# Prompt attention in 30 steps beside the samples' pages; keys transposed by VectorE in 32x32 blocks, scores in twelve 32x32 tiles at once

## The reference, cut to what matters

```python
# prompt: 512 queries, 512 keys
sc = einsum('bqhd,bkhd->bhqk', qi, k) * scale
sc = sc + ci[..., :, None] - c_k[:, :, None, :]          # c: running sum of log forget values
p = softmax(where(causal, sc, NEG_INF)); out = einsum('bhqk,bkhd->bqhd', p, v)
# sample: 8 queries, 2048 past keys in 16 pages of 128, found by a page table, and 8 new ones
r_past = cumsum(lf_past, reverse=True) - lf_past
s_past = einsum('bqhd,bkhd->bhqk', q, k_past) * scale + cq[..., :, None] + r_past[:, :, None, :]
p = softmax(concatenate([s_past, s_new], -1))
out = einsum('bhqk,bkhd->bqhd', p, concatenate([v_past, v]))
```

## Time and profile before

| | us |
|---|---|
| median of 3 runs | 2106.8 (2106.39 to 2113.93) |
| span of the profiled execution | 2106.6 |
| TensorE busy | 1840.3 (87%) |
| VectorE busy | 982.8 (47%) |
| ScalarE busy | 537.1 (25%) |
| GpSimd busy | 172.2 (8%) |
| TensorE in the chain that ended last | 74% of the span |
| DMA, mean over the span | 106 GB/s |

### The profile page before, as it was taken

How to read it: one execution, slowest core, us unless ns; L and a number is a source line. 1 busy time by engine, 2 the same in 40 slices (tenths; PEclk the granted TensorE clock), 3 DMA queues, 4 the chain that set the end, 5 groups by cost and what they waited for, 6 DMA issues and landing times.

```text
span 2106.6 us, 36927 instructions
## 1 busy us (share of the span) xinstructions
PE 1840.3 (87%) x13959; PEld 1610.9 (76%) x13959; DVE 982.8 (47%) x1689; ACT 537.1 (25%) x880; POOL 172.2 (8%) x332
## 2 busy tenths in 40 slices
PE   5999466899999999799766788888878899999998
PEld 4876345799999999699634456566557799999997
DVE  5396965533333222776457864444433533333222
ACT  3210233322222111433222323222312322222110
POOL 1010000000000000444100001122220000000000
PEclk9999867999999999999878769999988999999999
DMA  3210121222222322223421027788873222223221
GB/s 113 63 38 30 40 76 61 59 80 85 84 80 81 95 83 71 64 75 87 159 91 61 1 84 276 283 290 312 302 231 97 60 80 86 83 80 91 83 82 58
DMA packets 231243, 224.30 MB, mean 106 GB/s; under 512 B 12114, under 2 KB 199588, under 8 KB 231162
## 3 DMA queue, kind: packets, MB, share of 16 engines
q1 hardware_dynamic: 210736, 150.49, 23.1%
q0 software_dynamic: 19008, 69.43, 9.5%
q10 hardware_dynamic: 1418, 3.29, 0.5%
HBM read 215.37 MB, written 7.80 MB: 106 GB/s over the span
## 4 chain that ended last, share of the span: by engine, by line
PE 74%; DVE 14%; ACT 4%; DMA 3%; issue 3%; POOLq 0%; ACTq 0%; DVEq 0%; POOL 0%
PE ps L1335 54%; PE ps L1708 5%; PE ps L1544 3%; DMA vring<-in_cache_fox_v_dram 3%; PE ps L1720 2%; PE ps L1317 2%; PE ps L1746 2%; DVE tmp L382 1%; DVE stat L468 1%; PE ps L1725 1%; ACT prob L1046 1%; DVE prob L459 1%; DVE prob L494 1%; DVE yc L687 1%; DVE aL L386 1%
## 5 line engine op out<-in xcount | busy, mean ns | idle before, releaser
L1335 PE MATMUL ps<-aH,wH 128*128 128x288 f32 x2224 | 487.5, 301 | 51.8 <-DVE aL L386 34.6
L1335 PE MATMUL ps<-aL,wH 128*128 128x288 f32 x2224 | 480.3, 298 | 0.0
L1335 PE MATMUL ps<-aH,wL 128*128 128x288 f32 x2224 | 479.9, 298 | 0.0
L1335 PEld LDWEIGHTS ps<-aH,wH 128*128 128x128 f32 x2224 | 361.9, 191 | 61.2 <-issue 39.1
L363 DVE TENSOR_TENSOR wL<-raw,wH 128x1024 fp32r<-128x1024 f32 (+1 forms) x179 | 232.0, 1296 | 337.0 <-ACT wH L985 333.9
L1335 PEld LDWEIGHTS ps<-aL,wH 128*128 128x128 f32 x2224 | 362.3, 191 | 0.0
L1335 PEld LDWEIGHTS ps<-aH,wL 128*128 128x128 f32 x2224 | 362.2, 191 | 0.0
L985 ACT ACTIVATE wH<-raw 128x1024 fp32r<-128x1024 f32 (+1 forms) x179 | 198.8, 1111 | 386.6 <-PE ps L1335 358.1
L1335 PE MATMUL ps<-gH,wH 128*128 128x288 f32 x704 | 151.1, 296 | 4.8 <-DVE gL L605 4.8
L1335 PE MATMUL ps<-gH,wL 128*128 128x288 f32 x704 | 151.1, 295 | 0.0
L1335 PE MATMUL ps<-gL,wH 128*128 128x288 f32 x704 | 150.9, 295 | 0.0
(11 more groups left out here) (295 smaller groups left out, 1982.8 us busy)
## 6 DMA issues: line engine op xcount, KB each, us to landing
kring<-in_cache_fox_k_dram SPq DMA_DIRECT2D x128, 384.0 KB, 4.7
vring<-in_cache_fox_v_dram POOLq DMA_DIRECT2D x128, 384.0 KB, 5.2
raw<-in_w_gate_up_dram SPq DMA_DIRECT2D x88, 512.0 KB, 3.8
raw<-in_w_down_dram SPq DMA_DIRECT2D x32, 704.0 KB, 4.6
raw<-in_fox_w_in_dram SPq DMA_DIRECT2D x21, 512.0 KB, 3.9
raw<-in_w_out_dram SPq DMA_DIRECT2D x16, 512.0 KB, 3.8
raw<-in_conv_w_in_dram SPq DMA_DIRECT2D x14, 512.0 KB, 3.9
raw<-in_w_mem_kv_dram SPq DMA_DIRECT2D x8, 512.0 KB, 3.4
```

Source lines behind the costliest of these rows:

```text
L1335: mm = nc.tensor.matmul(ps[:, 2 * slot + h, 0:HT], weights[:, w], a[:, k0 + k, h * HT:(h + 1) * HT], start=(first and k == 0 and weights i ...
```

## The change

The prompt's 24 units become 30 steps (`fox_step`): a step has one head e and one or two parts, so that its scores always fill one bank of 512 columns: query tile 3 alone, tiles 0 and 2 of a head together, tile 1 of two heads together. The samples' 64 chunks become 32 slots of two chunks (512 keys, a quarter of a sample). Step s stands beside slot s in the order of every engine. All loops over samples are written out.

The keys are transposed by VectorE from SBUF to SBUF in 32x32 blocks (`KT`, two chunks to a slot, double), so TensorE's key transposes and both engines' copies out of PSUM go. A block has 32 channels, so a head is two blocks; partition group a holds the keys 32a to 32a + 31 of each page. `qx4` holds the queries in each of the four partition groups; scores are twelve tiles of 32x32, row group a and column group j, each into bank a, for 128 keys a tile; the forget rows follow as 32x32 tiles. All 2048 scores of a sample stay in the four banks 0 to 3: VectorE takes the maximum there, ScalarE's exponential reads them and writes S, and only then does the next sample's first slot write there. Banks 6 and 7 are taken in turn, in one order for all uses (`TURNS`). ScalarE takes over the copies of pT, pTs, the scaling and the queries (`spread`); GpSimd makes the forget rows (`forget_rows`) between its value loads; the forget stage stands beside the memory units (`forget(i)`). Both rings have three chunks.

```diff
-    RING = 4
+    RING = 3
+    SLOTS = NB * NCH // 2
+    SPB = SLOTS // NB
+    SPG = 2 * CPG
+    DQ = DH // 2
+    NBLK = CH // DQ
+    STEPS = 5 * HP
...
-    FOX_UNITS = [("fox", hp, t, (t + 1) * P) for hp in range(HP) for t in range(TT)]
+    def fox_step(i):
+        two, k = divmod(i, 5)
+        e, hp = two % 2, two - two % 2
+        parts = ([(0, 3, 0, SEQ)], [(1, 3, 0, SEQ)], [(0, 0, 0, P), (0, 2, P, 3 * P)], [(1, 0, 0, P), (1, 2, P, 3 * P)],
+                 [(0, 1, 0, 2 * P), (1, 1, 2 * P, 2 * P)])[k]
+        return k, e, [(n, hp + n, t, col, keys) for n, t, col, keys in parts]
...
+            def forget(i):
+                if i == 0:
+                    dve.wait_ge(lf_in, 16 * NB * NP)
+                    nc.vector.tensor_reduce(lftot[:], lfrow[:].rearrange("n (k h) -> n h k", h=NH), AX_X, ALU.add).then_inc(lftot_done, 1)
+                if i < 2 * (NH // 4):
+                    g = i % (NH // 4)
+                    bank = group()
...
+            def keys_T(s):
+                if s >= 2:
+                    dve.wait_ge(sc_done, s - 1)
+                for x in range(2):
+                    n = 2 * s + x
+                    dve.wait_ge(k_in[n % RING], 32 * (n // RING + 1))
+                    nc.vector.transpose(KT[s % 2][:, CPG * x:CPG * x + CPG, :].rearrange("p a n -> p (a n)"),
+                                        kring[n % RING][:].rearrange("p a n -> p (a n)")).then_inc(kt_done, 1)
...
+            def step_top(i):
+                k, e, parts = fox_step(i)
+                st = stat[:, 8 * (i % 2):8 * (i % 2) + 8]
+                pr = prob[:, i % 2, :]
+                if k == 0:
+                    for n in range(2):
+                        wait_taken(dve, ("ncb", i // 5, n))
+                dve.wait_ge(f_scores, i + 1)
+                for n, hp, t, col, keys in parts:
+                    last = nc.vector.scalar_tensor_tensor(out=pr[:, col:col + keys], in0=ps[:, 5, col:col + keys],
+                                                          scalar=ctok[:, t, 2 * hp + e:2 * hp + e + 1], in1=ncb[:, n, 0:keys],
+                                                          op0=ALU.add, op1=ALU.add)
+                link(last)
+                if k < 2:
+                    diagonal = pr[:, SEQ - P:SEQ]
+                    link(nc.vector.tensor_tensor(diagonal, diagonal, maskd[:], ALU.add))
+                else:
+                    first, by = (0, 3) if k < 4 else (1, 2)
+                    diagonal = pr.rearrange("p (a n) -> p a n", n=P)[:, first:TT:by, :]
+                    link(nc.vector.tensor_tensor(diagonal, diagonal, maskd[:].unsqueeze(1).broadcast_to([P, 2, P]), ALU.add))
+                for x, (n, hp, t, col, keys) in enumerate(parts):
+                    last = nc.vector.tensor_reduce(st[:, x:x + 1], pr[:, col:col + keys], AX_X, ALU.max, negate=True)
+                last.then_inc(f_max, 1)
+            def step_sums(i):
+                st = stat[:, 8 * (i % 2):8 * (i % 2) + 8]
+                dve.wait_ge(f_exp, i + 1)
+                nc.vector.reciprocal(st[:, 4:6], st[:, 2:4]).then_inc(f_rec, 1)
...
+            def sample_top(b):
+                wait_turn(dve, ("new", b))
+                nc.vector.tensor_tensor(S[:, NPAST:NPAST + NS], turn_bank(("new", b))[0:ROWS, 0:NS],
+                                        mshift[:, NS - NQ - NQ * b:2 * NS - NQ - NQ * b], ALU.add).then_inc(taken(("new", b)), 1)
+                wait_taken(dve, ("new", b))
+                link(nc.vector.tensor_reduce(stat[0:ROWS, 55:56], S[:, NPAST:NPAST + NS], AX_X, ALU.max, negate=True))
+                dve.wait_ge(sc_done, SPB * (b + 1))
+                link(nc.vector.tensor_reduce(stat[0:ROWS, 54:55], ps[0:ROWS, 0:4, :].rearrange("p a n -> p (a n)"), AX_X, ALU.max, negate=True))
+                link(nc.vector.scalar_tensor_tensor(out=stat[0:ROWS, 56:57], in0=stat[0:ROWS, 54:55], scalar=stat[0:ROWS, 55:56],
+                                                    in1=cqr[:, b:b + 1], op0=ALU.min, op1=ALU.subtract))
+                nc.vector.tensor_tensor(stat[0:ROWS, 56:57], stat[0:ROWS, 56:57], cqr[:, b:b + 1], ALU.add).then_inc(smax_done, 1)
...
+            keys_T(0)
+            for s in range(SLOTS + SPB):
+                b, cc = divmod(s, SPB)
+                if cc == 0 and b:
+                    sample_top(b - 1)
+                    if s <= STEPS:
+                        step_lo(s - 1)
+                if s < STEPS:
+                    step_top(s)
+                if s + 1 < SLOTS:
+                    keys_T(s + 1)
+                if s < STEPS:
+                    step_sums(s)
+                if cc == 0 and b:
+                    sample_sum(b - 1)
+                elif 1 <= s <= STEPS:
+                    step_lo(s - 1)
+                if cc == 1 and b >= 2:
...
+            def spread(b):
+                if b:
+                    act.wait_ge(sc_done, SPB * b)
+                    wait_turn(act, ("new", b - 1))
+                for m in range(4):
+                    nc.scalar.activation(qx4[:].rearrange("p (j m c) n -> p j m c n", m=4, c=2)[:, :, m, :, NQ * m:NQ * m + NQ],
+                                         qr[:].rearrange("p (j m) c n -> p j m c n", m=4)[:, :, m, :, NQ * b:NQ * b + NQ], ACT.Copy)
...
+            def sample_exp(b):
+                act.wait_ge(smax_done, b + 1)
+                nc.scalar.activation(S[:, 0:NPAST].rearrange("p (g a i) -> p a g i", a=4, i=DQ),
+                                     ps[0:ROWS, 0:4, :].rearrange("p a (g i) -> p a g i", i=DQ), ACT.Exp, bias=stat[0:ROWS, 56:57],
+                                     accum_out=stat[0:ROWS, 57:58])
+                nc.scalar.activation(S[:, NPAST:NPAST + NS], S[:, NPAST:NPAST + NS], ACT.Exp, bias=stat[0:ROWS, 56:57],
+                                     accum_out=stat[0:ROWS, 58:59]).then_inc(sexp_done, 1)
+                for g in range(4):
+                    n = min(5, NP - 5 * g)
+                    bank = turn_bank(("PT", b, g))
+                    wait_turn(act, ("PT", b, g))
+                    last = nc.scalar.activation(pTs[:, 5 * g:5 * g + n, :].rearrange("p k r -> p (k r)"), bank[:, 0:n * ROWS], ACT.Copy)
+                    if g == 3:
...
+                if 1 <= s <= STEPS:
+                    step_probT(s - 1)
+                if cc == 0 and b:
+                    if b >= 2:
+                        sample_scale(b - 2)
+                    if b < NB:
+                        spread(b)
+                    if s <= STEPS:
+                        step_hi(s - 1)
+                    sample_exp(b - 1)
+                if s < STEPS:
+                    step_exp(s)
+                if cc == 1 and b >= 2:
+                    sample_hi(b - 2)
+                if not (cc == 0 and b) and 1 <= s <= STEPS:
+                    step_hi(s - 1)
+                if s < STEPS:
+                    step_scale(s)
...
+            def slot_scores(s):
+                b, cc = divmod(s, SPB)
+                pe.wait_ge(kt_done, 2 * s + 2)
+                if cc == 0:
+                    pe.wait_ge(qx_done, b + 1)
+                    if b:
+                        pe.wait_ge(sexp_done, b)
+                k4 = KT[s % 2]
+                def out(a, j):
+                    return ps[QR * j:QR * j + QR, a, cc * P:(cc + 1) * P]
+                for m in range(4):
+                    for c in range(2):
+                        for a in range(4):
+                            for j in range(3):
+                                blk, r = 2 * (4 * j + m) + c, slice(DQ * a, DQ * a + DQ)
+                                nc.tensor.matmul(out(a, j).rearrange("p (g i) -> p g i", g=SPG), qx4[r, blk, :], k4[r, :, blk * DQ:blk * DQ + DQ],
+                                                 start=(m == 0 and c == 0), stop=False, skip_group_check=True, tile_position=(DQ * a, QR * j))
+                pe.wait_ge(rx_done, s + 1)
+                for g in range(SPG):
+                    for a in range(4):
+                        for j in range(3):
+                            r = slice(DQ * a, DQ * a + DQ)
+                            mm = nc.tensor.matmul(out(a, j)[:, g * DQ:(g + 1) * DQ], rx[r, g, 4 * j:4 * j + 4, :].rearrange("p h q -> p (h q)"),
+                                                  ident[r, DQ * a:DQ * a + DQ], start=False, stop=(g == SPG - 1), skip_group_check=True,
+                                                  tile_position=(DQ * a, QR * j))
+                mm.then_inc(sc_done, 1)
...
+            c_keys(0)
+            step_scores(0)
+            for s in range(SLOTS + SPB):
+                b, cc = divmod(s, SPB)
+                step = 1 <= s <= STEPS
+                if step:
+                    step_probT(s - 1)
+                if cc == 0 and b:
+                    if step:
+                        step_values(s - 1)
+                    sample_probT(b - 1)
+                if s < SLOTS:
+                    slot_scores(s)
+                    if cc == SPB - 1:
```

(82 more changed lines are left out.)

555 lines of the change are left out of this document (226 added, 329 removed).

## The result

The changed kernel takes 2176.9 us (median of 4 runs, 2162.55 to 2182.9) against 2106.75 of the kernel before: a ratio of 1.030, 95% interval 1.0255 to 1.0343. It is slower by 3%, where 1984 us was predicted. The profiled execution has a span of 2181.3 us; the projection starts at 1667.0 us instead of 1595.1, and what lies behind it takes 514.3 us (511.5 before).

A forecast was written before the change was run, and what follows sets the result against it. Bound before: a four-engine chain without traffic (prompt), traffic beside nearly full TensorE (samples). Projection start 1113.7 + 32 + 297.5 + 29 = 1472.2, 122.9 us earlier, gives 1984 us from 2106.6; forecast's own range 1940 to 2035.

The forecast's parts named there:

- the sum of a slot on TensorE: TensorE's work per slot: probT, scores with forget rows, values, step values and step scores, 6.9 us, with switches 7.3.
- Record rate: Rival: TensorE's rate for a slot's 288 score and forget records sets the time; totals 2018 to about 2570; chance 0.08.
- The rival's 4.75 us: Record-rate rival's lowest price for a slot's 288 records, at 0.0165 us each: sample 47.4 us, total 2018; whole rival's chance 0.08.
- until slot 3's scores end: Start of the changed part: memset, first keys, top, next keys, reciprocal and scale, then three slots at 7.0 us: 32 us.
- seven samples: Seven sample boundaries at 42.5 us each, three plain slots of 8.6 and one first slot of 16.7: 297.5 us.
- tail: End before the projection: exponential and transposes 6.5, last eight value chunks 19.5, output 3: 29 us.
- The range's upper end: Plain slots of 10.5 us, put at 314 GB/s, and 18 at the boundary: sample 49.5 us, total 2033.
- The boundary: First slot of a sample, which can't overlap because ScalarE must empty all four score banks first: 16.7 us.
- The forget rows: Forget stage beside the memory units: VectorE's sum and six passes end the units 7.3 us later; prompt work starts at 1113.7.
- the chain of a step: From scores' end through top, next keys' transposes, reciprocal, scale and waits: 7.0 us, hidden beside TensorE's next slot if over 7.
- One of the rivals' times, 2166: Rival in `slot_scores`: the four row groups don't run beside one another, scores 9.1 us instead of 2.6; chance 0.11.
- The rival at a rate of 0.025: Record-rate rival's middle case: 7.2 us for a slot's 288 records, plain slot 11.9, total 2094; whole rival's chance 0.08.

The follow-up runs named there:

- the looped run: Changed kernel with a quarter of each slot's score and forget-row matmuls run four times in a TensorE loop, three quarters of the scores left out: 2065.3 us.
- the run with both edits: Changed kernel with forget rows added by 12 matmuls per slot instead of 48, and score matmul groups set between the value matmuls: 2058.1 us, 0.976 of the kernel before.

## Why the prediction was wrong

**The step that failed is the sum of a slot on TensorE.** It counted the time of records, at full clock, and never asked how fast instructions come in. The plain slot at 1408.87, term by term:

| us | forecast | measured |
|---|---|---|
| score and forget records | 2.6 | 4.04 |
| idle inside them | 0 | 3.28 |
| values of two chunks | 1.7 | 3.12 |
| step values | 1.05 | 1.90 |
| step scores and transposes | 1.5 | 1.65 |
| sum | 7.3 with switches | 13.99 |

The idle for instructions is the largest part of the miss, and it costs twice. Value matmuls of a chunk lasted 0.86 us in the kernel before; here one chunk lasts 1.86 and step values 1.90 instead of 1.05: the granted clock over the slot is 0.76. In the looped run's plain slot, where the same matmuls stand without idle, it is 1.00, and the values and step values take 3.0 us together instead of 5.0. So the clock is 2.0 us, and idle and clock together are 5.3 of the 6.7.

The Trainium skill (Runtime: NRT & Kernel Launch, Instruction fetch mechanics) states that instructions are fetched in blocks of 256 while the current block runs, and that this is mostly hidden. The trace agrees on the 256 and not on the hiding: 96.8 us lie open.

**Record rate.** 288 records in 4.04 us are 0.0140 us each, between the 0.011 and the 0.0165 of the prediction, and more than the 3.2 us that it took as a bound without any overlap. The 2.6 was 1.4 us per slot too small: a burst on twelve tiles does not run like one on three. In the run with both edits, at full clock, 48 records of 32x128 take 0.87 us (1383.99 to 1384.86), 0.22 for a burst of twelve where 0.113 was taken. The rival's 4.75 us came nearer; what limits such a burst was not tried.

**Over the whole part**, start and ends of slots from the timeline:

| | forecast | measured | too long by |
|---|---|---|---|
| prompt work starts | 1113.7 | 1121.1 | 7.4 |
| until slot 3's scores end | 32 | 50.1 | 18.1 |
| seven samples | 7 x 42.5 | 7 x 65.7 | 162.7 |
| tail | 29 | 35.6 | 6.6 |
| from the projection on | 511.8 | 514.3 | 2.5 |

That is the 197.3 us between 1984 and the profiled 2181.3. The range's upper end has a slip besides: 3.15 MB at 314 GB/s are 10.0 us and not 10.5, and with it the range would have ended some 10 us lower.

*The boundary* was 16.7; slots that hold one average 23.6 us in the changed kernel and 19.3 in the run with both edits. Its chain of work is near the forecast (TensorE waits 24.6 us over eight samples for the exponential, 3.1 each, where some 4 were forecast). In the changed kernel 3.3 us of the 23.6 are stops for instructions. In the run with both edits the slot behind a boundary has a clock of 0.75 to 0.89; what else makes up the 2.6 us over the forecast is open. With 9.9 us for the mean plain slot, that run stays at 49.6 us per sample instead of 42.5, and at 2058 instead of 1984.

*The forget rows* were priced at the sum and six passes of VectorE, 7.3 us. The start moved by 14.7 (1121.1 less 1106.4), but 6.4 of that stands ahead of the change: the copy of pT of the first memory unit, before and now.

```profile
1060.68 0.69 DVE L502 COPY pT<-ps 128x512 f32<-128x512 f32 x1 [1.21 <-PE ps L1317]
1067.10 0.69 DVE L541 COPY pT<-ps 128x512 f32<-128x512 f32 x1 [1.21 <-PE ps L1446]
```

Over all the profiles here, the same point of this untouched work lies up to 7 us apart. From it to the start of the prompt work it is 8.3 us longer than before, so the 7.3 was nearly right, and nearly all of the 7.4 us in the table's first row isn't the change's. Within it two errors cancel in part. VectorE's copies of the triangle products wait for TensorE, whose eight products of two records stand in the unit's chain:

```profile
1085.31 0.69 DVE L904 COPY rtok<-ps 128x512 f32<-128x512 f32 x1 [1.21 <-PE ps L1802]
...
1089.33 0.69 DVE L904 COPY rtok<-ps 128x512 f32<-128x512 f32 x1 [1.21 <-PE ps L1802]
```

Such a unit takes 4.02 us instead of 2.50, 1.52 more where 0.75 was forecast for a pass; a unit whose pass does not wait takes 2.74, only 0.24 more.

**What was right.** The key transposes and the maximum over four banks, groups of VectorE:

```profile
L922 DVE STREAM_TRANSPOSE KT<-kring 128x1536 f32<-128x1536 f32 x64 | 109.8, 1753 | 0.4 <-DMA kring<-in_cache_fox_k_dram 0.3
...
L971 DVE TENSOR_REDUCE stat<-ps 96x1 f32<-96x2048 f32 x8 | 18.3, 2286 | 0.3
```

1.753 us for the forecast 1.75, though the trace of before had no such transpose. Rings of three hardly starve (7.6 us of waits for values, 0.3 for keys), and the chain of a step hides (4.8 us of waits for pT in all). The sign turned on the supply of instructions: with it eased and the work whole, 2058 us.

One of the rivals' times, 2166, fell near the measured one, and that was luck: the row groups overlap. The rival at a rate of 0.025, 2094, isn't what the trace shows either; the rate inside the bursts is 0.014.

## What to carry to other kernels

Count a stretch's instructions per microsecond on an engine, not only their durations: here a block of 256 followed the one before at 3.4 us at the least, more often near 5, so written-out bursts that use one up in 2 us wait. Idle that is put to "issue", with 256 or 512 instructions between stops, is the sign of it; a loop, fewer and larger instructions, or longer ones between the small take it away (here 112, 88 and 50 us). And where the stops went, the clock of a plain slot rose (0.76 to 1.00 in the looped run).

## What the runs showed of the hardware

- A block of instructions is a packet of 16 KB and 256 instructions of TensorE. In the changed kernel two packets never began less than 3.4 us apart, and TensorE went on 1.2 to 1.6 us after one had landed; between two stops with 256 instructions between them 3.4 to 6.5 us passed, and 3.5 to 6.2 with half the pages' traffic.
- A loop of some 850 TensorE instructions ran without a new block per pass (52 packets), and the same passes written out took 17 more.
- Twelve 32x32 tiles ran beside one another at 0.014 us per record; three tiles of one row group at a time took 7.9 us for the same 288 records instead of 4.0.
- In that run TensorE was busy all of a slot (14.40 of 14.40 us) and yet granted 0.76 of its clock, while the run with both edits, busy all of a slot too, was granted 1.00. What makes the difference was not tried.
- A 32x32 block transpose of 128x1536 float32 from SBUF to SBUF took VectorE 1.753 us.
